# Row weights carried with the dispatched rows, adding gathers, and a last tile by column halves

## The reference

```python
def moe_swiglu(h, w_router, w_gate, w_up, w_down):
    logits = (h @ w_router).astype(jnp.float32)
    top_vals, top_idx = lax.top_k(logits, TOP_K)          # TOP_K = 2
    top_w = jax.nn.softmax(top_vals, axis=-1)
    combine = jnp.einsum('bsk,bske->bse', top_w,
                         jax.nn.one_hot(top_idx, N_EXPERTS, dtype=jnp.float32)).astype(h.dtype)
    out = jnp.zeros_like(h)
    for e in range(N_EXPERTS):
        out = out + combine[..., e:e + 1] * swiglu(h, w_gate[e], w_up[e], w_down[e])
    return out
# x = x + moe_swiglu(rmsnorm(x, od_norm_ffn), ...);  return rmsnorm(x, final_norm)
```

## Time and profile before

| | us |
|---|---|
| median of 3 runs | 1716.88 (1712.34 to 1717.13) |
| profiled execution | 1714.35 |
| its span, first to last instruction | 1712.5 |
| PE busy | 1673.8 (98%) |
| DVE busy | 1416.5 (83%) |
| ACT busy | 1124.6 (66%) |
| POOL busy | 180.3 (11%) |
| mean granted TensorE clock | 0.992 |

### The profile page before, as it was taken

How to read it: one execution, slowest core, us unless ns; L and a number is a source line. 1 busy time by engine, 2 the same in 40 slices (tenths; PEclk the granted TensorE clock), 3 DMA queues, 4 the chain that set the end, 5 groups by cost and what they waited for, 6 DMA issues and landing times.

```text
span 1712.5 us, 26271 instructions
## 1 busy us (share of the span) xinstructions
PE 1673.8 (98%) x10142; PEld 1477.5 (86%) x10142; DVE 1416.5 (83%) x1392; ACT 1124.6 (66%) x1128; POOL 180.3 (11%) x164
## 2 busy tenths in 40 slices
PE   9999999999999999999999999999999999999996
PEld 8888999999999998887888888888888888888885
DVE  7997789857876657778888888888888888888888
ACT  5326578753554446677777777777777777777775
POOL 5000355412400011020000000000000000000300
PEclk9999999999999999999999999999999999999998
DMA  8335699994455555369999999999999999999993
GB/s 332 123 123 204 148 227 335 348 260 173 173 197 197 197 197 156 148 224 423 401 380 387 367 382 390 363 390 383 367 387 388 374 386 368 389 384 354 408 421 139
DMA packets 75614, 513.50 MB, mean 300 GB/s; under 512 B 8368, under 2 KB 8848, under 8 KB 17424
## 3 DMA queue, kind: packets, MB, share of 16 engines
q1 hardware_dynamic: 68832, 487.13, 74.7%
q0 software_dynamic: 6560, 25.31, 5.6%
q10 hardware_dynamic: 144, 0.00, 0.0%
HBM read 488.27 MB, written 24.14 MB: 299 GB/s over the span
## 4 chain that ended last, share of the span: by engine, by line
PE 85%; DVE 8%; ACT 3%; DMA 2%; issue 1%; SPq 0%; DVEq 0%; ACTq 0%
PE psum L764 26%; PE psum L766 26%; PE psum L765 26%; DVE wlo L1684 3%; PE psum L817 3%; DMA wraw<-weights 2%; PE psum L1202 1%; DVE acc L1768 1%; ACT whi L1279 1%; PE psum L1170 0%; PE psum L904 0%; ACT whi L1617 0%; ACT s L1504 0%; PE psum L856 0%; DVE zc L1989 0%
## 5 line engine op out<-in xcount | busy, mean ns | idle before, releaser
L1684 DVE TENSOR_TENSOR wlo<-wraw,whi 128x2048 fp32r<-128x2048 f32 (+1 forms) x446 | 1014.8, 2275 | 192.8 <-ACT whi L1617 108.5
L1617 ACT ACTIVATE whi<-wraw 128x2048 fp32r<-128x2048 f32 x336 | 645.2, 1920 | 226.8 <-PE psum L766 217.7
L764 PE MATMUL psum<-whi,xgh 128*128 128x512 f32 x896 | 354.0, 395 | 2.4 <-DVE wlo L1684 1.5
L766 PE MATMUL psum<-whi,xgl 128*128 128x512 f32 x896 | 349.9, 391 | 0.0
L765 PE MATMUL psum<-wlo,xgh 128*128 128x512 f32 x896 | 348.8, 389 | 0.0
L764 PE MATMUL psum<-ah,whi 128*128 128x256 f32 x1048 | 293.5, 280 | 4.6 <-issue 2.4
L765 PE MATMUL psum<-al,whi 128*128 128x256 f32 x1048 | 290.8, 277 | 0.0
L766 PE MATMUL psum<-ah,wlo 128*128 128x256 f32 x1048 | 290.7, 277 | 0.0
L1279 ACT ACTIVATE whi<-wraw 128x2048 fp32r<-128x2048 f32 x104 | 198.8, 1913 | 113.4 <-PE psum L766 104.2
L764 PEld LDWEIGHTS psum<-ah,whi 128*128 128x128 f32 x1048 | 197.7, 189 | 5.2 <-issue 2.1
L764 PEld LDWEIGHTS psum<-whi,xgh 128*128 128x128 f32 x896 | 168.2, 188 | 36.8 <-DVE wlo L1684 1.9
(11 more groups left out here) (343 smaller groups left out, 2177.8 us busy)
## 6 DMA issues: line engine op xcount, KB each, us to landing
wraw<-weights SPq DMA_DIRECT2D x453, 1024.0 KB, 4.9
expert_rows<-zeros POOLq DMA_DIRECT2D x1, 8704.0 KB
expert_outs<-zeros POOLq DMA_DIRECT2D x1, 4608.0 KB
expert_outs<-ysb SPq DMA_DIRECT2D x8, 512.0 KB, 6.6
xgt<-expert_rows SPq DMA_DIRECT2D x8, 512.0 KB, 5.6
bias_rows<-ttab POOLq DMA_DIRECT2D x1, 3072.0 KB, 36.6
btab<-bias_rows POOLq DMA_DIRECT2D x4, 384.0 KB, 9.5
xres<-x SPq DMA_DIRECT2D x1, 1024.0 KB, 4.9
```

The source lines that it names most:

```text
L764: nc.tensor.matmul(out, lh, rh, start=start, stop=False)
L766: return nc.tensor.matmul(out, ll, rh, start=False, stop=stop)
L1617: sc.activation(whi[:, (GS + j) % NS, :], wraw[:, g % NW, :], ACT.Copy).then_inc(hi_done, 1)
L1684: return ve.tensor_tensor(dst, value, hi.bitcast(f32), SUB)
```

## The change

Four edits. (1) `hrow` gets a third extra column, the weight of the choice. POOL writes the weights of choice 0, scatters both tiles, waits for both, writes the weights of choice 1 and scatters again. SP loads each expert's column into `wslot` before granule 16, with the wait for `dispatched` ahead of the first such load, and ACT scales the expert's result by it as it copies to `ysb`. (2) The gathers add into the token rows `xtm` in SBUF (`compute_op=ADD`), those of choice 1 behind those of choice 0 of the same tile; `yrow1`, `yrow2` and the four `choice` sums go. (3) VectorE's residual for granule 1 of an expert moves from the end of the previous pass to the start of its own (`low(1)`), so that behind the last expert none is made. (4) The end goes by column halves: in the last granule of an expert TensorE does all products of bank 4 first and tells so by `half_used`; ACT copies half 0 then, half 1 when all are done, and loads the table after; picks, sums, the last result and its store are by halves.

```diff
-DW = D + 2
+DW = D + 3
@@ SP
+                    if j == 16:
+                        sp.wait_ge(dispatched, 64)
+                        sp.dma_start(wslot[:], rows_in[bass.ds(E * P + P, P), D + 1:DW]).then_inc(share_loaded, 16)
                     if j == 30:
-                        sp.wait_ge(dispatched, 64)
                         sp.wait_ge(xgt_mm, E * 2 + 2)
...
-            for t in range(2):
-                sp.wait_ge(fin_out, t + 1)
-                sp.dma_start(out_d[t * P:(t + 1) * P, :], outb[:, t, :]).then_inc(stored, 16)
-            sp.wait_ge(stored, 32)
+            sp.wait_ge(fin_out, 1)
+            sp.dma_start(out_d[0:P, :], outb[:, 0, :]).then_inc(stored, 16)
+            for n in range(2):
+                sp.wait_ge(fin_out, n + 2)
+                sp.dma_start(out_d[P:2 * P, n * 512:(n + 1) * 512], outb[:, 1, n * 512:(n + 1) * 512]).then_inc(stored, 16)
+            sp.wait_ge(stored, 48)
@@ POOL
-            for t in range(2):
-                for r in range(2):
+            for r in range(2):
+                if r:
+                    pool.wait_ge(dispatched, 32)
+                pool.wait_ge(shares_ready, r + 1)
+                nc.gpsimd.tensor_copy(hrow[:, :, D + 2], wrow[:, 2 * r:2 * r + 2]).then_inc(shares_in, 1)
+                pool.wait_ge(shares_in, r + 1)
+                for t in range(2):
                     i = 2 * t + r
                     pool.indirect_dma_start(out=rows_in, out_offset=bass.IndirectOffsetOnAxis(ap=idx[:, i:i + 1], axis=0),
                                             in_=hrow[:, t, :], in_offset=None).then_inc(dispatched, 16)
             pool.wait_ge(dispatched, 64)
             pool.wait_ge(rows_ready, 1)
-            for t in range(2):
-                for r, dst in enumerate((yrow1, yrow2)):
+            pool.wait_ge(xtm_out, 4)
+            for r in range(2):
+                for t in range(2):
                     i = 2 * t + r
-                    pool.indirect_dma_start(out=dst[:, t, :], out_offset=None, in_=rows_out,
-                                            in_offset=bass.IndirectOffsetOnAxis(ap=idx[:, i:i + 1], axis=0)
-                                            ).then_inc(row_back[i], 16)
+                    if r:
+                        pool.wait_ge(row_back[2 * t], 16)
+                    pool.indirect_dma_start(out=xtm[:, t, :], out_offset=None, in_=rows_out,
+                                            in_offset=bass.IndirectOffsetOnAxis(ap=idx[:, i:i + 1], axis=0),
+                                            compute_op=ADD).then_inc(row_back[i], 16)
@@ PE
+                    by_half = c == FC - 1 and half == 1
+                    for i, n in ((0, 0), (1, 0), (0, 1), (1, 1)) if by_half else ((0, 0), (0, 1), (1, 0), (1, 1)):
...
+                        if by_half and (i, n) == (1, 0):
+                            mm.then_inc(half_used, 1)
...
+            for n in range(2):
+                pe.wait_ge(last_lo, n + 1)
+                w = slice(n * 512, (n + 1) * 512)
+                for t in range(2):
+                    pe.wait_ge(last_ready, t + 1)
                     nc.tensor.matmul(bank[2 * t + n], last[:, t, :], ylh[:, w], start=True, stop=False)
+                    nc.tensor.matmul(bank[2 * t + n], last[:, t, :], yll[:, w], start=False, stop=True).then_inc(picked, 1)
@@ ACT
+                act.wait_ge(share_loaded, E * 16 + 16)
                 for n in range(2):
-                    sc.activation(ysb[:, n * 512:(n + 1) * 512], bank[4 + n], ACT.Copy).then_inc(y_out, 1)
+                    sc.activation(ysb[:, n * 512:(n + 1) * 512], bank[4 + n], ACT.Copy, scale=wslot[:, 1:2]).then_inc(y_out, 1)
...
+                act.wait_ge(half_used, passes)
+                sc.activation(ylh[:, 0:512], bank[4], ACT.Copy).then_inc(last_hi, 1)
+                act.wait_ge(parts_used, passes * PARTS + PARTS)
+                sc.activation(ylh[:, 512:1024], bank[5], ACT.Copy).then_inc(last_hi, 1)
...
-                sc.activation(tabled[:], ident[:, 0:1], ACT.Sqrt)
-                act.wait_ge(parts_used, NE * PARTS + PARTS)
+                last_high(NE)
+            sc.activation(tabled[:], ident[:, 0:1], ACT.Sqrt)
@@ DVE
+            ve.memset(wslot[:], 0.0).then_inc(share_loaded, 16)
...
             inputs_lo(0, 0)
-            split_ahead(1)
             inputs_lo(0, 1)
...
+                low(1)
                 for j, (kind, c, half) in enumerate(MOE):
...
-                    v.wait_ge(hi_done, E * BODY + (i + 1))
-                    lo(wlo[:, i % NS, :], wraw[:, g % NW, :], whi[:, i % NS, :]).then_inc(lo_done, 1)
+                    if j + 2 <= BODY:
+                        low(j + 2)
...
-            choice(0, 0)
-            choice(0, 1)
             for n in range(2):
                 v.wait_ge(last_hi, n + 1)
                 w = slice(n * 512, (n + 1) * 512)
                 lo(yll[:, w], bank[4 + n], ylh[:, w]).then_inc(last_lo, 1)
             v.wait_ge(gains_loaded, 32)
-            choice(1, 0)
...
+            def half_row(t, n):
+                v.wait_ge(row_back[2 * t + 1], 16)
+                v.wait_ge(picked, 2 * n + t + 1)
+                w = slice(n * 512, (n + 1) * 512)
+                ve.scalar_tensor_tensor(xtm[:, t, w], bank[2 * t + n], comb[:, t, NE - 1:NE], xtm[:, t, w], MUL, ADD
                                         ).then_inc(added, 1)
...
+                for w in (slice(0, D),) if t == 0 else (slice(0, 512), slice(512, D)):
+                    ve.scalar_tensor_tensor(outb[:, t, w], xtm[:, t, w], rs[:, 14 + t:15 + t], fgain[:, w], MUL, MUL
+                                            ).then_inc(fin_out, 1)
-            whole_row(0)
-            choice(1, 1)
-            whole_row(1)
+            for t in range(2):
+                for n in range(2):
+                    half_row(t, n)
             spread_of(0)
             row_result(0)
             spread_of(1)
```

## The result

The changed kernel took 1701.19 us (median of 7 runs, 1698.35 to 1704.16) against 1714.08 for the kernel before on the same chip: ratio 0.9931, 95% interval 0.9913 to 0.9948. It is faster, as forecast, but the time lies 8.8 us under the forecast of 1710.0 and 3.8 under the range. The profiled execution took 1699.79, its span is 1697.8: 14.7 us less than before, where 5.6 were forecast.

What follows compares the result with a forecast made beforehand. TensorE, busy 1673.8 of 1712.5 us, was taken as the bound, with gains only where it stands still, chiefly the 18.5 us tail. 6.4 - 0.3 - 0.5 = 5.6 us saved gave 1710.0 us, range 1705 to 1715.5.

Steps and rivals of the forecast that it cites:

- Tail: Behind the last expert product: unused residual and row sums leave VectorE, work goes by halves; gain 6.4 us, bounds 4.8 to 7.2.
- The output: Last store in the tail: 256 KB instead of 512 KB lands sooner; gain 0.6 us, bounds 0 and 1.2.
- First expert: Paired scatters and SP's earlier wait just hidden; cost 0.3 us including small loads, bounds -0.3 and +2.
- Rival 2: First expert: SP's earlier wait starves it, granule 16 late by up to 2 us; gain about 4, 1712 us, chance 0.13.
- Adding gathers: Last expert: adding gathers, two plus two, stall TensorE by 0.5 us, taken between 0 and 1.3.
- Rival 1: Last expert: adding gathers read twice and TensorE stalls 1.3 us; gain 4.8, 1711 us, chance 0.2.
- the doubled case: Last expert: an adding gather costs twice a plain one, 4.9 - 3.6 = 1.3 us of stall.
- Small load, memset, residual moved: Loop edits: moved residual costs 0, memset and other semaphores 0 to 0.2 us; small loads share the scatters' 0.3 us.
- Rivals 3 and 4: Tail not shortened by its sums, gain 3 to 4, chance 0.1; adding gathers over three times plain, 1720, chance 0.08.

Runs made afterwards that it cites:

- e1_width: Kernel before with one more float in each row, cleared and unused (pitch 4108 B instead of 4104 B): 1704.70 us against 1716.95, ratio 0.9931.
- width_copy: Kernel before with only the row widened by one float, profiled again in the fifth group: 1705.04 us, ratio 0.9922.
- e6_vector_sums: Changed kernel with plain gathers and the four sums, without weights, back on VectorE in the tail: 1701.76 us, ratio 0.9915 to before.
- e4_at_once: Changed kernel with one copy of weights and its four scatters sent at once, choice 1 carrying choice 0's weight: 1700.93 us, ratio 0.9909 to before.
- e2_pairs: Kernel before with its four scatters in two pairs, the second sent when the first has landed: 1717.88 us, ratio 1.0005.
- e7_narrow: Changed kernel at the old row width (1026 columns, pitch 4104 B), the weight taking one of the two columns: 1712.06 us, ratio 0.9967 to before.
- after: The changed kernel as first measured and profiled: 1701.19 us against 1714.08 for the kernel before, ratio 0.9931.
- after_copy: The changed kernel, unchanged, profiled again in the fifth group: 1700.77 us, ratio 0.9901 to the kernel before.
- after_again: The changed kernel run once more in the second group: 1700.00 us, ratio 0.9898 to the kernel before.
- e5_pool_sums: Changed kernel with plain gathers into two buffers and the four sums made by POOL in the last expert: 1709.71 us, ratio 0.9963 to before.

## Why the prediction was wrong

The direction was right and the tail's mechanism was right; the time was 8.8 us off because one edit was never priced. The sum has a term for each wait, copy and sum, and none for `DW = D + 3`: the prediction doesn't mention the wider row, and so puts it at nothing without a reason. The 4 bytes more are nothing, but the distance between rows is a property of every write to `expert_rows`, and there it was worth 12 us on two chips (e1_width, width_copy).

The rows could have raised it. The earlier trace rows give the chain 16.14 us in a weight load in the first expert, and the earlier trace rows give 14.3 us for a scatter of 512 KB, in a stretch where the DMA is full at 307 and 371 GB/s (the windows above) and not at the 425 of the earlier trace rows. The prediction took that as the load of four scatters at once; in e1_width the same scatter, also one of four at once, lands in 10.6, so by these traces 3.7 us of it were the price of the row that it wrote to. And it never looked at the zero fill, which the same width touches.

Point by point:
- **Tail, 6.4 forecast, 7.3 found.** Last result 8.77 us behind the last product (1695.34 - 1686.57), 8.7 forecast; the clock stayed at 1.00 through all eight picking products, 0.23 us apart from the second on; the mean comes with no wait behind the half sums. `yll` half 0 is ready at 1687.01, 0.4 us behind the last product and not 0.6. The half sums took 0.74 us each and not 0.65, and the halves of the result 0.71: halves are dearer than half. The output is the term that was mis-sized: 256 KB land in 2.1 us, so 1.5 us were saved and not 0.6, past the bound of 1.2 (with which the tail's upper bound would be 7.0, and not 7.2 as written). By e6_vector_sums the sums gave 3.3 of it.
- **First expert, cost 0.3 forecast.** The pairs cost nothing at the new width (e4_at_once). The step was right in its answer and wrong in its numbers: POOL's copy took 1.88 and 1.45 us, not 0.20, and the last scatter landed at 767.3, which is 772.7 on the forecast's scale and not 776.7. SP issued granule 16 at 768.04 and it was split at 775.11. Rival 2 didn't come, but thanks to the width that nobody had priced: at the old width the stage is 1.9 us longer with the pairs alone (e2_pairs) and 3.1 with SP's earlier wait too (e7_narrow), in one trace each. That is what the rival feared and more. The medians neither confirm nor exclude it.
- **Adding gathers, 0.5 forecast, 1.5 to 2.5 found.** Rival 1's mechanism was right: twice the DMA time. Its price of 1.3 us was low by some 0.7 (120.09, 120.56, 120.90 and 121.10 against 118.64; 121.56 at the old width). TensorE's own waits in the traces of after, after_copy and after_again are 0.6, 1.2 and 1.7 us and name VectorE, since ACT's late split reaches TensorE by way of the residual. I should have taken the doubled case and not half the distance to it.
- **Small load, memset, residual moved: 0.** The six experts take 711.84 us in every kernel. ACT's scaled copies of a result took 676 ns each, the plain ones 585, so scaling did take time there, and no stage shows it.
- **Rivals 3 and 4** fell: the tail is shorter by all it was to be, and an adding gather costs about two plain ones and not three.
- Without the width the number stands: 5.6 us against 4.8 in e7_narrow [3.4 to 7.7] and 4.3 in after_copy against width_copy. Part of that is luck: the tail gave 0.9 to 1.2 more than forecast, the gathers took 1.0 to 2.4 more, and at the old width the scatters took up to 2.8 more.

Open: why in 240 to 270 us, with rows 4104 bytes apart, the DMA moves 209 to 237 GB/s, and with rows of 4108, 4112, 4120, 4136 and 4160 bytes 416 to 421; and why with the same 4104 bytes it moves 424 and 393 in other parts of the fill. In the column fill the width also changes the piece from 8 to 12 bytes, and no run sets one apart from the other; in the row fill the piece is 4096 bytes in all, so there only the distance is left. Also open: why one chip ran the kernel before at 1708.22.

## What to carry to other kernels

A constant that sets the distance between rows in HBM is an edit of its own: price it at every DMA that writes such rows, and look for windows with the DMA share at 1 and the bandwidth well under what full share gives elsewhere in the trace. Try one or two other paddings before building on a layout. An add in the DMA takes no engine time and cost its bytes about twice here, so where weights stream at full rate try such gathers one at a time (0.35 us of stall instead of 1.5 to 2.5). Sums moved to GpSimd beside a VectorE that subtracts from SBUF can stop VectorE for their whole length (e5_pool_sums).

## What the hardware showed unexpectedly

- Rows of 4104 bytes: 209 to 237 GB/s at full DMA share in 240 to 270 us, against 416 to 421 for five other widths, but 424 in 230 to 235 of the same fill. While 17 KB in columns of 8 bytes were filled, ACT waited 5.1 us for a weight load. Traces from several chips show both; one chip ran the kernel before at 1708.22, and no trace of the old width was taken on it.
- GpSimd's copy of 128x2 took 1.88 and 1.45 us, 0.70 in e7_narrow, and a like one of 128x4 0.20 us. What makes the difference isn't shown.
- VectorE's residual took 11.49 us beside GpSimd's sums, five times its 2.29. The Trainium skill (SBUF — State Buffer, Who interferes with whom) says that a VectorE instruction with two SBUF inputs contends with a GpSimd one that reads SBUF, and the trace agrees: one residual stood through all 9.33 us of sums.
- A stretch between the same two TensorE instructions can differ by 3.6 us between executions of one kernel (114.49 in e1_width and 118.09 in width_copy, from instruction 1500 to 2500), and others by 2 to 5; it is why single profiled executions, such as e7_narrow's 1718.91 beside its median of 1712.06, mislead.
